# Expert loop of a mixture-of-experts layer: matmuls grouped by PSUM bank, the first bias in four row groups, the second matrix loaded in 8 KB pieces

## The reference, cut to what matters

```python
logits = ht @ w_router + b_router
top_v, top_i = lax.top_k(logits, 4)
gate = softmax(top_v)
# tokens are sorted by expert into blocks, one expert per block
gu   = xb @ w_gu[e] + b_gu[e]                  # [block, 1024] @ [1024, 2048]
g    = minimum(gu[:, :1024], 7)
lin  = clip(gu[:, 1024:], -7, 7)
act  = g * sigmoid(1.702 * g) * (lin + 1)
y    = act @ w_down[e] + b_down[e]             # [block, 1024] @ [1024, 1024]
out[token] += gate * y
```

## Time and profile before

| | |
|---|---|
| time, 3 runs | 1600.45 us median, 1597.85 to 1601.16 |
| profiled execution | 1601.96 us, span 1600.1 us (first to last instruction) |
| granted PE clock, mean | 0.994 of full speed (2.4 GHz) |
| PE busy | 1570.5 us, 98% |
| DVE busy | 1282.4 us, 80% |
| ACT busy | 1084.5 us, 68% |
| DMA | 466.97 MB, 292 GB/s over the span, about 370 GB/s in the job loop |

### The profile page before, as it was taken

How to read it: one execution, slowest core, us unless ns; L and a number is a source line. 1 busy time by engine, 2 the same in 40 slices (tenths; PEclk the granted TensorE clock), 3 DMA queues, 4 the chain that set the end, 5 groups by cost and what they waited for, 6 DMA issues and landing times.

```text
span 1600.1 us, 21816 instructions
## 1 busy us (share of the span) xinstructions
PE 1570.5 (98%) x7658; PEld 1143.4 (71%) x7658; DVE 1282.4 (80%) x1018; ACT 1084.5 (68%) x999; POOL 423.0 (26%) x265
## 2 busy tenths in 40 slices
PE   8999999999899999999999999999999999999997
PEld 7866688888766777777777777777777777777774
DVE  3768734337699998999899899998998999989884
ACT  6368723223467777877777778777777877777773
POOL 0000260000022722223443222234432222343220
PEclk9999999999899999999999999999999999999999
DMA  7310022337299999999999999999999999999984
GB/s 271 111 59 22 11 86 88 123 119 291 104 376 337 366 365 377 374 360 378 372 358 371 361 381 378 367 368 374 356 368 369 367 378 372 367 369 362 375 304 138
DMA packets 102565, 466.97 MB, mean 292 GB/s; under 512 B 13288, under 2 KB 13824, under 8 KB 69728
## 3 DMA queue, kind: packets, MB, share of 16 engines
q1 hardware_dynamic: 94416, 448.71, 73.5%
q0 software_dynamic: 7776, 17.68, 5.2%
q10 hardware_dynamic: 336, 0.08, 0.0%
HBM read 456.82 MB, written 19.27 MB: 298 GB/s over the span
## 4 chain that ended last, share of the span: by engine, by line
PE 92%; DVE 5%; issue 1%; DMA 1%; ACT 0%; DVEq 0%; POOL 0%; ACTq 0%; POOLq 0%
PE ps L1752 28%; PE ps L1770 14%; PE ps L1755 14%; PE ps L1775 7%; PE ps L1449 6%; PE ps L1451 6%; PE ps L1450 6%; PE ps L1476 4%; PE ps L1744 2%; DVE l_w L1196 1%; PE ps L1602 1%; DVE head_max L1125 1%; PE ps L1558 1%; DVE probs L1143 1%; PE ps L1679 1%
## 5 line engine op out<-in xcount | busy, mean ns | idle before, releaser
L817 ACT ACTIVATE h_w<-a_w 128x2048 fp32r<-128x2048 f32 x384 | 731.3, 1915 | 235.7 <-PE ps L1755 170.2
L1196 DVE TENSOR_TENSOR l_w<-a_w,h_w 128x2048 fp32r<-128x2048 f32 x384 | 865.4, 2290 | 31.0 <-ACT h_w L817 29.1
L971 POOL TENSOR_TENSOR mark_sb<-ones 1x1 f32<-1x1 f32 x93 | 245.9, 2644 | 727.5 <-ACT y_sb L865 718.7
L1752 PE MATMUL ps<-h_w,xt_hi 128*96 128x512 f32 x1024 | 287.4, 402 | 2.3 <-DVE xt_lo L1335 2.3
L1752 PE MATMUL ps<-h_w,xt_lo 128*96 128x512 f32 x1024 | 279.2, 394 | 0.0
L1755 PE MATMUL ps<-l_w,xt_hi 128*96 128x512 f32 x1024 | 278.0, 393 | 0.0
L1752 PEld LDWEIGHTS ps<-h_w,xt_lo 128*96 128x96 f32 x1024 | 166.1, 162 | 71.7
L1755 PEld LDWEIGHTS ps<-l_w,xt_hi 128*96 128x96 f32 x1024 | 165.4, 162 | 71.2
L1752 PEld LDWEIGHTS ps<-h_w,xt_hi 128*96 128x96 f32 x1024 | 163.6, 162 | 70.8 <-ACT h_w L817 1.7
L1770 PE MATMUL ps<-h_w,at_hi 128*96 128x512 f32 x512 | 162.1, 398 | 0.2 <-issue 0.2
L1770 PE MATMUL ps<-h_w,at_lo 128*96 128x512 f32 x512 | 159.5, 392 | 0.0
(11 more groups left out here) (252 smaller groups left out, 1555.5 us busy)
## 6 DMA issues: line engine op xcount, KB each, us to landing
a_w<-in_w_gate_up SPq DMA_DIRECT2D x256, 1024.0 KB, 7.2
a_w<-in_w_down SPq DMA_DIRECT2D x128, 1024.0 KB, 6.7
w_raw<-in_w_in SPq DMA_DIRECT2D x8, 2048.0 KB, 7.9
w_raw<-in_w_out SPq DMA_DIRECT2D x2, 2048.0 KB, 7.6
w_raw<-in_w_in SPq DMA_DIRECT2D x2, 1024.0 KB, 7.7
x_sb<-in_x SPq DMA_DIRECT2D x8, 256.0 KB, 7.0
w_raw<-in_w_mem_kv SPq DMA_DIRECT2D x1, 2048.0 KB, 11.0
x<-in_x SPq DMA_DIRECT2D x4, 512.0 KB, 5.2
```

What stands on the lines that cost most here:

```text
L817: nc.scalar.activation(h_w[m % H_SLOTS][:], a_w[m % A_SLOTS][:], ACT.Copy).then_inc(wh_done, 1)
L971: nc.gpsimd.tensor_tensor(mark_sb[:], ones[0:1, 0:1], ones[0:1, 0:1], ALU.mult).then_inc(marked, 1)
L1196: nc.vector.tensor_tensor(l_w[m % A_SLOTS][:], a_w[m % A_SLOTS][:], h_w[m % H_SLOTS][:].bitcast(F32), ALU.subtract).then_inc(wl_done, 1)
L1752: nc.tensor.matmul(ps[0:SLOTS, n, :], x_part[:, k, :], w_h[:, n * COLS:(n + 1) * COLS], start=False, stop=False)
```

## The change

Three edits, all in the job loop.

1. **Order of matmuls.** In `gate_up` and `down` the three products of a bank follow each other: `xt_hi` x `h_w`, `xt_hi` x `l_w`, `xt_lo` x `h_w`, then the next bank. PE now waits for the low part ahead of all 12 matmuls of a part, not ahead of the last four. The number of matmuls stays.
2. **First bias.** The table is no longer three bfloat16 pieces in 96 rows but two fp32r parts (`bias_hi`, `bias_lo`) in which the four blocks of 512 columns lie in partition groups 0-31, 32-63, 64-95 and 96-127. The bias of bank n is a matmul of 32 rows of group n, once with the high and once with the low table: 8 matmuls of 32 rows and not 4 of 96. The one-hot tiles have 128 rows (four copies of the 32 experts), and the preparation on POOL is shorter.
3. **Second matrix.** Row block k of `w_down` is now every 8th row, beginning with k, and no longer rows 128k to 128k+127. Partition p so takes rows 8p to 8p+7, and the two rows of a part are one piece of 8 KB. For the transposed activations to fit, the activations are written in permuted order: L851, L1344 and L1350 write (and L1350 also reads) SBUF with a step of 128 elements, 512 bytes, from one element to the next, while they read PSUM in sequence.

```diff
-            bias_pieces = [(bias_gu[:, 0:D], b_gate_up[0][:, 0:D]), (bias_gu[:, D:2 * D], b_gate_up[0][:, D:2 * D])]
...
+            for n in range(4):
+                pool.dma_start(bias_f[N_EXP * n:N_EXP * (n + 1), :], b_gate_up[0][:, n * COLS:(n + 1) * COLS]).then_inc(bias_in, 16)
+            pool.wait_ge(bias_in, 64)
+            step.link(nc.gpsimd.tensor_copy(bias_hi[:], bias_f[:]))
+            step.link(nc.gpsimd.tensor_tensor(bias_lo[:], bias_f[:], bias_hi[:].bitcast(F32), ALU.subtract))
...
-        wdn = w_down[0].rearrange("e (k p) n -> e p k n", p=P)
+        wdn = w_down[0].rearrange("e (p k) n -> e p k n", p=P)
...
+        def by_down_row(t):
+
+            return t.rearrange("s (k h p) -> s h p k", k=KD, h=2)
+
+        def of_bank_pair(n):
+            return ps[0:SLOTS, n:n + 2, :].rearrange("s h (p k) -> s h p k", k=KD)
...
-                nc.scalar.activation(sg_sb[:].rearrange("p (h n) -> p h n", h=2), ps[0:SLOTS, 0:2, :], ACT.Relu, bias=limits[0:SLOTS, 0:1],
+                nc.scalar.activation(by_down_row(sg_sb[:]), of_bank_pair(0), ACT.Relu, bias=limits[0:SLOTS, 0:1],
...
-                nc.vector.tensor_scalar(act_sb[:].rearrange("p (h n) -> p h n", h=2), ps[0:SLOTS, 2:4, :], LIMIT, -LIMIT,
+                nc.vector.tensor_scalar(by_down_row(act_sb[:]), of_bank_pair(2), LIMIT, -LIMIT,
...
-                sg = sg_sb[:].rearrange("p (h n) -> p h n", h=2)
-                nc.vector.scalar_tensor_tensor(out=sg, in0=ps[0:SLOTS, 0:2, :], scalar=LIMIT, in1=sg,
+                sg = by_down_row(sg_sb[:])
+                nc.vector.scalar_tensor_tensor(out=sg, in0=of_bank_pair(0), scalar=LIMIT, in1=sg,
...
-            nc.vector.tensor_scalar(y_sb[:].rearrange("p (h n) -> p h n", h=2), ps[0:SLOTS, 0:2, :], LIMIT, None, ALU.min).then_inc(gs_ready, 1)
+            nc.vector.tensor_scalar(by_down_row(y_sb[:]), of_bank_pair(0), LIMIT, None, ALU.min).then_inc(gs_ready, 1)
...
-                for n in range(4):
-                    nc.tensor.matmul(ps[0:SLOTS, n, :], expert_gu[:], bias_gu[:, n * COLS:(n + 1) * COLS], start=True, stop=False)
+                for part in (bias_hi, bias_lo):
+                    for n in range(4):
+                        rows = slice(N_EXP * n, N_EXP * (n + 1))
+                        nc.tensor.matmul(ps[0:SLOTS, n, :], expert_gu[rows, :], part[rows, :], start=part is bias_hi, stop=False)
...
-                    for x_part in (xt_hi, xt_lo):
-                        for n in range(4):
-                            nc.tensor.matmul(ps[0:SLOTS, n, :], x_part[:, k, :], w_h[:, n * COLS:(n + 1) * COLS], start=False, stop=False)
                     wait_low(pe, i, m)
                     for n in range(4):
-                        last = nc.tensor.matmul(ps[0:SLOTS, n, :], xt_hi[:, k, :], w_l[:, n * COLS:(n + 1) * COLS], start=False, stop=k == KD - 1)
+                        bank, c = ps[0:SLOTS, n, :], slice(n * COLS, (n + 1) * COLS)
+                        nc.tensor.matmul(bank, xt_hi[:, k, :], w_h[:, c], start=False, stop=False)
+                        nc.tensor.matmul(bank, xt_hi[:, k, :], w_l[:, c], start=False, stop=False)
+                        last = nc.tensor.matmul(bank, xt_lo[:, k, :], w_h[:, c], start=False, stop=k == KD - 1)
```

More of the change, by code:

```diff
@@ L274, in encoder_kernel @@
         sum_row = small("sum_row", [SLOTS, 2], I32)
-        job_hot_b = small("job_hot_b", [96, NJ], BF16)
-        expert_gu = small("expert_gu", [96, SLOTS], BF16)
+        job_hot_b = small("job_hot_b", [P, NJ], F32)
+        expert_gu = small("expert_gu", [P, SLOTS], F32R)
         row_miss = small("row_miss", [SLOTS, NJ], F32)
@@ L837, in name_gu @@
             def name_gu(j):
-                nc.scalar.activation(expert_gu[:], job_hot_b[:, bass.ds(j, 1)].to_broadcast([96, SLOTS]), ACT.Copy).then_inc(expert_gu_ready, 1)
+                nc.scalar.activation(expert_gu[:], job_hot_b[:, bass.ds(j, 1)].to_broadcast([P, SLOTS]), ACT.Copy).then_inc(expert_gu_ready, 1)
             def take_xt(j):
@@ L997, in _ @@
             pool.wait_ge(marked, 2)
-            step.link(nc.gpsimd.memset(expert_gu[:], 0.0))
-            for g in range(3):
-                nc.gpsimd.memset(expert_gu[N_EXP * g:N_EXP * g + 1, :], 1.0).then_inc(first_expert, 1)
-            pool.wait_ge(first_expert, 3)
+            step.link(nc.gpsimd.memset(expert_gu[:].bitcast(F32), 0.0))
+            for n in range(4):
+                nc.gpsimd.memset(expert_gu[N_EXP * n:N_EXP * n + 1, :].bitcast(F32), 1.0).then_inc(first_expert, 1)
+            pool.wait_ge(first_expert, 4)
             pool.wait_ge(row_0_ready, 1)
@@ L1710, in _ @@
             stay_awake(4)
-            pe.wait_ge(blocks_ready, 3)
+            pe.wait_ge(blocks_ready, TB)
             turn(1, 0, blocks_end[:].rearrange("p g e -> p (g e)"))
@@ L1766, in down @@
                     wait_high(pe, i, m)
-                    for k in range(2):
-                        for a_part in (at_hi, at_lo):
-                            for n in range(2):
-                                nc.tensor.matmul(ps[0:SLOTS, 4 + n, :], a_part[:, 2 * q + k, :], w_h[:, (2 * k + n) * COLS:(2 * k + n + 1) * COLS],
-                                                 start=q == 0 and k == 0 and a_part is at_hi, stop=False)
                     wait_low(pe, i, m)
@@ L1774, in down @@
                         for n in range(2):
-                            last = nc.tensor.matmul(ps[0:SLOTS, 4 + n, :], at_hi[:, 2 * q + k, :], w_l[:, (2 * k + n) * COLS:(2 * k + n + 1) * COLS],
-                                                    start=False, stop=q == DN_PARTS - 1 and k == 1)
+                            bank, c = ps[0:SLOTS, 4 + n, :], slice((2 * k + n) * COLS, (2 * k + n + 1) * COLS)
+                            nc.tensor.matmul(bank, at_hi[:, 2 * q + k, :], w_h[:, c], start=q == 0 and k == 0, stop=False)
+                            nc.tensor.matmul(bank, at_hi[:, 2 * q + k, :], w_l[:, c], start=False, stop=False)
+                            last = nc.tensor.matmul(bank, at_lo[:, 2 * q + k, :], w_h[:, c], start=False, stop=q == DN_PARTS - 1 and k == 1)
                     last.then_inc(gemm_ps, 1)
```

39 lines of the change are left out of this document (13 added, 26 removed).

## The result

| | before | changed |
|---|---|---|
| time, 17 runs each | 1601.16 us median (1597.85 to 1604.3) | 1604.81 us median (1602.88 to 1608.68) |
| profiled execution | 1601.96 us | 1603.28 us, span 1601.4 us |

The changed kernel takes 1.002 times as long, with a 95% interval from 1.0012 to 1.0027, which is 3.2 us (1.9 to 4.3). The forecast was 1585.5 us; 1604.8 lies above its range.

What follows compares the result with a forecast made beforehand. The prediction took PE's pace in the job loop as the bound. Order -15.4, bias -1.0 and the permuted writes' exposed cost +1.4 summed to -15.0 us, from 1600.45 to 1585.5 us, range 1580 to 1603.

Steps and rivals of the forecast that it cites:

- What bounds the kernel: Job loop: PE, busy for all of 560 to 1500 us at full clock, sets the pace of 35.46 us a pass.
- Edit 1, the order: gate_up and down: new order brings settled matmuls from 230.9 to 226.7 ns, 0.48 us a pass, 15.4 us in all.
- the two differences that the step had put aside: Loop against front part: stationary operand of 96 columns, not 128; bank change after 3 matmuls, not 12 or 24.
- Rival one: Loop matmuls: pace stays at 231 ns because 96 columns or bank change set it; 1601 us, no change; chance 0.27.
- never falls below 230.9: Argument for unchanged pace: even the loop's settled part, 60 matmuls without a break, stays at 230.9 ns or above.
- Earlier wait for the low part: Loop: costs nothing, as DVE works some 19 us ahead; without that cover, 1.85 us a part.
- Edit 2, the bias: First bias: 1.07 us instead of 1.10, mode change included; gain 0.03 us a pass, 1 us in all.
- Edit 3, price: Permuted activation writes: 0.7 ns an element more, 0.7 us each for L1344 and L1350, the same on ACT's L851.
- In the loop it costs nothing. It is exposed once: Permuted writes: DVE's idle time absorbs them in the loop; only the start of job 1 pays, +1.4 us.
- 8 KB pieces: Loads of down: worth nothing by themselves, but 422 instead of 407 GB/s guards the new pace.
- the floor: DMA need per pass: some 34.7 us with 4 KB pieces, 34.3 with 8 KB, below the new pass of 34.95.
- Sum: Whole kernel: -15.4 - 1.0 + 1.4 = -15.0 us, median from 1600.45 to 1585.5 us.

Runs made afterwards that it cites:

- e1_order: The kernel before with only the new matmul order (three products per bank); ratio 1.0004 to the kernel before.
- p1_wide: The changed kernel with gate_up's stationary operand 128 columns wide, not 96, slices still 384 bytes apart; 1606.0 us, one execution.
- p2_wide_swept: The kernel before with gate_up's stationary operand 128 columns wide, not 96, slices still 384 bytes apart; 1602.3 us, one execution.
- g3_spaced: The changed kernel with stationary slices 512 bytes apart, not 384, but only their 96 columns read; 1599.7 us, one execution.
- g2_wide_spaced_swept: The kernel before with stationary operands 128 columns wide and slices 512 bytes apart; 1587.22 us, ratio 0.9898 (run again on another chip: 0.9930).
- d1_dve_1us: The changed kernel with one more DVE reduction of 1024 elements a pass, result unused; 1607.0 us, one execution.
- f1_psum_steps: The changed kernel with the permutation made by reading PSUM in 32-byte steps and writing SBUF in sequence; 1600.68 us, ratio 0.9992.

## Why the prediction was wrong, step by step

- **What bounds the kernel: right.** PE was the bound before and after, and what slowed it was its own pace.
- **Edit 1, the order: wrong, and the step that failed.** "I take 15.4, since order is the larger of the differences between the two places." The order alone gives 0.007 us a pass, 0.2 us in all, where 0.48 and 15.4 had been put (`e1_order`). What set 230.9 against 226.7 ns was one of the two differences that the step had put aside, the 96 columns, together with one that it had not seen, slices that begin at odd multiples of 128 bytes. Rival one named the columns, at 0.27; alone they give nothing (`p1_wide`, `p2_wide_swept`), and the place alone gives 0.12 us a pass (`g3_spaced`). Both together give what had been forecast for the order, 35.460 - 34.993 = 0.47 us a pass where 0.48 had been worked out (0.42 on the changed kernel). The cause was wrong, and that the size fits is partly luck: behind the three breaks of a pass of `g2_wide_spaced_swept` not 10 matmuls each are unsettled but 4, 0 and 10 (bias, activation and token transposes), and the first one behind each transposition takes 23 to 29 ns longer than before. The trace of before held the hint. Single starts in its even parts are 230.1 ns apart and in its odd ones 231.6; a mean over 56 matmuls hid it, and so it is not true that the settled part "never falls below 230.9", which stood for rival one.
- **Earlier wait for the low part: right.** No wait for `l_w` in the steady passes.
- **Edit 2, the bias: right.** From the last matmul of `down` to the first big one: 1006.65 - 2 x 0.231 - 1005.14 = 1.05 us, forecast 1.07. Four groups start within some 10 ns, the second round 0.30 us behind the first (forecast 0.33), the mode change ahead takes 0.33 us (0.32). Gain 0.06 us a pass, forecast 0.03. That it shrinks to some 0.02 with 128 columns was not foreseen.
- **Edit 3, price: right in size.** 0.74 to 0.79 ns an element on DVE where 0.7 was taken from the reduction, and 0.97 on ACT.
- **Edit 3, "In the loop it costs nothing. It is exposed once": half right.** The steady margin is there (`d1_dve_1us`), and the start of job 1 costs 1.45 us where 1.4 was forecast, closer than this distance repeats from one execution to the next. But the step took the steady pass for all passes. In the first ones DVE has not caught up and has no margin (`d1_dve_1us`), and the edit was paid twice more: 1.0 us in the second distance, with a lower clock for 6.8 us instead of 3.4, and 0.65 us in the third, with the wait for `xt_lo`. Of nine kernels with writes in 512-byte steps six had the long stretch of lower clock at job 1, of eleven others one; so it is likelier with them, but not set by them alone. In sum the steps cost the first three distances some 2 to 3 us, and `f1_psum_steps` gives them back.
- **8 KB pieces: right that they are worth nothing; the floor was not reached.** A pass of 34.99 us ran with 4 KB pieces and without a wait for a weight part. Whether 34.7 us is the floor stays open.
- **Sum.** Forecast -15.4 - 1.0 + 1.4, with 32 passes; only 28 of the 31 distances are steady. Measured in the profiles: -0.2 for the order, -1.5 for the bias, +3.1 for the start, together +1.4; the spans differ by 1.3, the timed executions by 3.2, and what makes up the rest stays open.

## What to carry to other kernels

When the same instruction runs at two paces in one trace, list everything that differs between the two places, operand addresses and widths too, and split the slow place by each before choosing: a mean over alternating parts hides the one that matters. Idle time of an engine covers extra work only in the passes in which it has it; look at the first passes by themselves, where a small lateness can also cost the clock. And where an operation must permute on its way from PSUM to SBUF, try both sides for the steps: here one side costs 60% (DVE) to 90% (ACT) more and the other nothing.
